# Attention on one core: the scores of two head pairs issued in a row, and value products that alternate between two PSUM banks in layers three and four

## The chip, the cores and the metric

The kernel runs on one core of one Trainium2 chip. The metric is the device time of one execution in microseconds (us); lower is better. The program is one launch, and its activations are only 256 tokens by 1024 columns, so most of its time goes to streaming and multiplying weights in TensorE.

## The reference

Two small transformer stacks are computed one after the other, four layers in all, on `x` of 1 x 256 x 1024 in fp32. The matrices around the attentions don't matter here. What matters is that each layer has attention over 256 tokens with heads of about 64 columns, and that this is computed per head:

```
s   = q @ k.T * scale + bias          # 256 x 256, causal or chunked
p   = exp(s - max(s))                 # row by row
out = (p @ v) / sum(p)
```

- Layer one ("nsa") has two branches of 16 heads each with one and the same mask (32 head jobs), and beside them a compressed branch. Each branch is weighted by a gate.
- Layer two ("dil") has 16 heads in three groups with three masks. The groups' weights come from the log sums of all heads.
- Layer three ("ab") has 8 heads with 96 rows of q and k (64 plain, 32 rotary), and then 8 heads of 64 with a sink in the denominator.
- Layer four ("cd") has 8 heads with 66 rows (64, and two that carry the forgetting decay), and then 8 heads of 64 with a bias table.

## The kernel before

Tokens lie in two tiles of 128. A head's scores are three blocks of 128 x 128 (the fourth is hidden by the mask), 384 columns in one PSUM bank. Heads go in pairs, and each engine has its own loop over pairs `p`:

- TensorE (`att_pe`, L611): scores of pair `p` (L641 and L643, `S` or `G0`/`G1` by the parity of `p`), transposes of pair `p-1`'s probabilities (`turn_probs`, L622, six of 128 x 128 in banks `T0`, `T1`), other work of the layer (`behind`), the value products of pair `p-2` (`times_v`, L630 to L632), and more work of the layer (`after`).
- VectorE (`att_dve`, L666): score plus bias with the row minimum of its negative, into one of four `scr` slots and `negmax` (L685, L687, "maxes"), then `between`, then the division of pair `p-2` by its sum (`take`: L2580 to L2588, L2248 to L2252, or L2242 to L2244), then `behind`.
- ScalarE (`att_act`, L708): the exponentials of pair `p` (L727, L728), `between`, then the copy of pair `p-1`'s transposes from PSUM (`copies`, L718), then `behind`.

A fp32 matmul is two instructions in the trace, so four stand for the scores of two heads. q and k of heads with 64 rows lie in one half of the partitions by the head's parity: the profile shows their matmuls as 64*128, those of the others as 96*128 or 66*128.

The order is held by semaphores. Scores of pair `p` wait for the maxes of pair `p-2`, which had the same banks. Maxes of pair `p` wait for the transposes of pair `p-2`, which had the same `scr` slots. The value products all go to bank `G2` (`out_bank`, L217; only the last pair but one uses `G3`), so those of a pair wait until `take` of the pair before is done (`att["outs"]`).

`G3` serves what `behind` and `after` bring in. In layer one these are the late parts of the modulation: L440 on TensorE, its sum on VectorE (L453), a spreading matmul (L446) and a copy on ScalarE (L458), in the iterations `LATE_AT = (2, 4, 7, 9, 11, 13)`; and the compressed branch: its maximum and probabilities on VectorE (L2552 to L2566), a transpose in iteration 5 (L1482, copied at L1999), and its outputs in `OUT_AT = (6, 8, 10, 12)` (L1493, L2574). ScalarE's `between` there scales a share of the late weights (L2015), and GpSimd adds them (L992). In its last iterations VectorE also splits the first quarter items of the next weights (L2609) from a copy by GpSimd (L1018), and GpSimd adds the branches (L986). Layer two has late parts in iteration 2 only. Layers three and four use `G3` in iterations 0 and 1 (`weave_turn`, L547).

Of the kernel before, what the change touches and what calls it, by code (L numbers as in the profile page):

```python
# [25 lines left out]
P = 128  # L26
D = 1024
T = 256
NT = T // P
KT = D // P  # L30
H = 16
# [24 lines left out]
SW = 3 * P  # L56
# [24 lines left out]
class Tally:  # L81
# [9 lines left out]
    def done(self, ins, sem=None):  # L91

        sem = self.own if sem is None else sem
        self.mark(ins, sem)
        self.eng.wait_ge(sem, self.n[sem.name] + (0 if self.turns is None else self.turns * self.per[sem.name]))
# [25 lines left out]
def over(ap, axis, n):  # L121

    a = ap.unsqueeze(axis)
    shape = list(a.shape)
    shape[axis] = n
    return a.broadcast_to(shape)


def two_stacks(nc, a, out):
    with ExitStack() as ctx:  # L130
# [83 lines left out]

        SB = [S, G[0:2]]

        def out_bank(name, p):  # L217

            return 3 if p == len(att_jobs[name]) // 2 - 2 else 2

        def att_out(name, j):
# [240 lines left out]
        turns = {}  # L462
# [145 lines left out]

        def att_pe(pe, name, behind=None, after=None, bank_free=None, mid=None):  # L611
            jobs, b0 = att_jobs[name], att_base[name]
            pairs = len(jobs) // 2

            def turn_probs(j):

                pe.wait_ge(att["probs"], 2 * (b0 + j) + 2)
                if j >= 2:

                    pe.wait_ge(att["turned"], b0 + j - 1)  # L620
                for b in range(3):
                    ins = pe.transpose(TB[j % 2][:, b * P:(b + 1) * P], scr[:, j % 4, 1 + b * P:1 + (b + 1) * P], ident)  # L622
                ins.then_inc(att["turns"], 1)

            def times_v(j):

                v = jobs[j][2]
                pe.wait_ge(att["turned"], b0 + j + 1)
                o, pt = att_out(name, j), probT[:, j % 4, :]
                pe.matmul(o[:, 0, :], pt[:, 0:P], v[0], start=True, stop=True)  # L630
                pe.matmul(o[:, 1, :], pt[:, P:2 * P], v[0], start=True, stop=False)  # L631
                pe.matmul(o[:, 1, :], pt[:, 2 * P:SW], v[1], start=False, stop=True).then_inc(att["pv"], 1)  # L632

            for p in range(pairs + 2):
                if p < pairs:
                    if p >= 2:

                        pe.wait_ge(att["maxes"], 2 * (b0 + 2 * (p - 1)))
                    two = [(jobs[2 * p + e][0], jobs[2 * p + e][1], SB[p % 2][e]) for e in range(2)]
                    for q, k, bank in two:  # L640
                        pe.matmul(bank[:, 0:P], q[:, 0:P], k[:, 0:P], start=True, stop=True)  # L641
                    for q, k, bank in two:
                        pe.matmul(bank[:, P:SW], q[:, P:T], k[:, 0:T], start=True, stop=True).then_inc(att["scores"], 1)  # L643
                if mid is not None:
                    mid(p)
                if p == pairs:
                    if bank_free is not None:
                        bank_free()
                    times_v(2 * p - 4)
                if 1 <= p < pairs + 1:  # L650
                    for j in (2 * p - 2, 2 * p - 1):
                        turn_probs(j)
                if p == pairs:
                    times_v(2 * p - 3)
                if behind is not None:
                    behind(p)
                if p >= 2 and p != pairs:
                    if p >= 3:

                        pe.wait_ge(att["outs"], b0 // 2 + min(p, pairs) - 2)  # L660
                    for j in (2 * p - 4, 2 * p - 3):
                        times_v(j)
                if after is not None:
                    after(p)

        def att_dve(dve, tl, name, bias_of, scale_of, take, sink=None, between=None, behind=None):  # L666
            done, TT = tl.done, dve.tensor_tensor
            jobs, b0 = att_jobs[name], att_base[name]
            n = len(jobs)
            for p in range(n // 2 + 2):  # L670
                for i in (2 * p, 2 * p + 1):
                    if i < n:
                        dve.wait_ge(att["scores"], b0 + i + 1)
                        if i >= 4:

                            dve.wait_ge(att["turns"], b0 + i - 3)
                        s, bank, bias, h = scr[:, i % 4, :], SB[p % 2][i % 2], bias_of(i), i % H
                        if i >= H:

                            dve.wait_ge(att["probs"], 2 * (b0 + i - H) + 2)  # L680
                        least, scale = 3e38, scale_of(i)
                        if sink is not None and sink(i) is not None:
                            least = sink(i)

                        tl.mark(dve.tensor_tensor_reduce(s[:, 1:1 + P], bank[:, 0:P], bias[:, 0:P], -scale, least, ALU.add, ALU.min,  # L685
                                                         negmax[:, h, 0:1]), att["maxes"])
                        tl.mark(dve.tensor_tensor_reduce(s[:, 1 + P:1 + SW], bank[:, P:SW], bias[:, P:SW], -scale, least, ALU.add, ALU.min,  # L687
                                                         negmax[:, h, 1:2]), att["maxes"])
                    if between is not None:
                        between(i)  # L690
                if sink is not None and 2 * p < n and sink(2 * p) is not None:
                    rows = slice(2 * p, 2 * p + 2)
                    dve.wait_ge(att["maxes"], 2 * (b0 + 2 * p + 2))
                    done(TT(den[:, rows, :], negmax[:, rows, :], over(sinks[:, 2 * p - 8:2 * p - 6], 2, NT), ALU.add), ab_s["sink_in"])
                if p >= 2:
                    dve.wait_ge(att["pv"], b0 + 2 * p - 2)
                    o, jobs_of = att_outs(name, p - 2), slice(2 * p - 4, 2 * p - 2)
                    rows = slice((2 * p - 4) % H, (2 * p - 4) % H + 2)
                    summed = o[:, :, :, DH:DH + 1]
                    if sink is not None and sink(2 * p - 4) is not None:  # L700
                        dve.wait_ge(ab_s["sink_exp"], p - 5)
                        summed = den[:, rows, :].unsqueeze(3)
                        done(TT(summed, summed, o[:, :, :, DH:DH + 1], ALU.add))
                    take(p - 2, o[:, :, :, 0:DH], summed, rden[:, jobs_of, :])
                if behind is not None:
                    behind(p)

        def att_act(act_, name, sink=lambda i: False, between=None, behind=None):  # L708
            n, b0 = len(att_jobs[name]), att_base[name]

            def copies(p):

                for j in (2 * p - 2, 2 * p - 1):
                    act_.wait_ge(att["turns"], b0 + j + 1)
                    if j >= 4:

                        act_.wait_ge(att["pv"], b0 + j - 3)
                    act_.copy(probT[:, j % 4, :], TB[j % 2][:, 0:SW]).then_inc(att["turned"], 1)  # L718

            for p in range(n // 2 + 1):  # L720
                if p == n // 2 - 1:
                    copies(p)
                for i in (2 * p, 2 * p + 1):
                    if i < n:
                        act_.wait_ge(att["maxes"], 2 * (b0 + i) + 2)
                        h, s = i % H, scr[:, i % 4, :]
                        act_.activation(s[:, 1:1 + P], s[:, 1:1 + P], ACT.Exp, bias=negmax[:, h, 0:1], scale=-1.0).then_inc(att["probs"], 1)  # L727
                        act_.activation(s[:, 1 + P:1 + SW], s[:, 1 + P:1 + SW], ACT.Exp, bias=negmax[:, h, 1:2],  # L728
                                        scale=-1.0).then_inc(att["probs"], 1)
                    if between is not None and i < n:  # L730
                        between(i)
                if p >= 1:
                    if p != n // 2 - 1:
                        copies(p)
                    if sink(2 * p - 2):
                        rows = slice(2 * p - 2, 2 * p)
                        act_.wait_ge(ab_s["sink_in"], p - 4)
                        act_.activation(den[:, rows, :], den[:, rows, :], ACT.Exp).then_inc(ab_s["sink_exp"], 1)
                if behind is not None:
                    behind(p)  # L740
# [2230 lines left out]
```

## Time and profile before

| What | us |
|---|---|
| median of 3 runs | 986.23 (985.34 to 986.41) |
| span of the profiled execution | 984.6 |
| attention of layer one | 108 to 182 |
| attention of layer two | 303 to 336 |
| attention of layer three | 412 to 441 |
| attention of layer four | 733 to 762 |

The span runs from the first to the last instruction; the page gives no time of the profiled execution beyond it, and the median of the runs is 1.6 us longer. In the views of the profile, PE is TensorE's matmuls and PEld its weight loads, DVE is VectorE, ACT ScalarE and POOL GpSimd. A row of a timeline has the start, the time from its first start to its last end, the engine and line, what is written from what, and in brackets the idle time before it with what ended it. Matmuls overlap in the pipeline: the step from one row's start to the next is what they cost, not the time in the second column.

### The profile page before, as it was taken

To read this page: it belongs to the slowest core of one execution; us is meant where nothing else is said; L and a number is where in the kernel's file an instruction comes from. 1 tells how busy PE (TensorE), PEld (TensorE's weight loads), DVE (VectorE), ACT (ScalarE), POOL (GpSimd) and SP (SyncE) were. 2 spreads that over 40 slices of the span, in tenths; PEclk is the share of its full clock that TensorE was granted. 3 is DMA by queue.
4 is the path that set the end of the run, shared out by engine and by line. 5 is a ranking of instruction groups with operands and counts; after the bars stand their busy time and mean duration, and the time that the engine had idled before them with its cause. 6 is when DMAs were issued, how large, how long until landed. Compare 5 with 4: busy or idle time off the path is not lost.

```text
span 984.6 us, 15103 instructions
## 1 busy us (share of the span) xinstructions
PE 954.9 (97%) x5656; PEld 806.3 (82%) x5656; DVE 645.7 (66%) x1164; ACT 471.4 (48%) x734; POOL 180.9 (18%) x154
## 2 busy tenths in 40 slices
PE   5999999999999999999999999999999999999996
PEld 2799666878886789988888888879999888888884
DVE  3656567975755775667766766676445776766665
ACT  1453577545445635573344444444457334444442
POOL 2015337204961301230000000010023000000001
PEclk9999999999999999999999999999999999999998
DMA  9865655435564255223465555534532336555541
GB/s 374 352 245 169 235 194 195 149 128 183 201 228 178 89 186 228 87 87 129 154 261 203 209 208 187 187 143 158 190 129 86 129 137 257 187 188 184 187 182 43
DMA packets 24105, 178.37 MB, mean 181 GB/s; under 512 B 3792, under 2 KB 4224, under 8 KB 7928
## 3 DMA queue, kind: packets, MB, share of 16 engines
q1 hardware_dynamic: 19840, 166.70, 45.4%
q0 software_dynamic: 2224, 8.94, 2.9%
q10 hardware_dynamic: 1991, 2.07, 0.8%
q8 instruction: 31, 0.51, 0.2%
q14 instruction: 19, 0.15, 0.0%
HBM read 176.65 MB, written 1.05 MB: 180 GB/s over the span
## 4 chain that ended last, share of the span: by engine, by line
PE 85%; DVE 9%; ACT 2%; DMA 2%; issue 1%; POOL 0%; SPq 0%; DVEq 0%; ACTq 0%; POOLq 0%
PE G L1109 12%; PE G L1111 12%; PE G L1110 12%; PE S L1229 8%; PE T L1229 8%; PE S L1228 4%; PE T L1228 3%; PE T L622 2%; PE T L527 2%; PE G L1309 2%; PE G L1298 2%; PE G L1290 2%; PE G L632 1%; PE G L631 1%; PE G L630 1%; DVE wlo L2174 1%
## 5 line engine op out<-in xcount | busy, mean ns | idle before, releaser
L2312 DVE TENSOR_TENSOR wlo<-ring,whi 128x2048 fp32r<-128x2048 f32 x88 | 154.4, 1758 | 88.4 <-ACT whi L1873 54.0
L1109 PE MATMUL G<-whi,hTh 128*128 128x308 f32 (+3 forms) x480 | 163.9, 341 | 0.5 <-DVE hTl L568 0.3
L1111 PE MATMUL G<-whi,hTl 128*128 128x308 f32 (+3 forms) x480 | 161.1, 336 | 0.0
L1110 PE MATMUL G<-wlo,hTh 128*128 128x308 f32 (+3 forms) x480 | 161.0, 336 | 0.0
L2174 DVE TENSOR_TENSOR wlo<-ring,whi 128x1024 fp32r<-128x1024 f32 (+3 forms) x66 | 105.4, 1635 | 64.9 <-ACT whi L1731 64.7
L1229 PE MATMUL S<-hT,whi 128*128 128x512 f32 x336 | 122.0, 397 | 0.0
L1229 PE MATMUL T<-hT,whi 128*128 128x512 f32 x336 | 120.6, 394 | 0.0
L1109 PEld LDWEIGHTS G<-whi,hTh 128*128 128x128 f32 x480 | 90.2, 188 | 11.2 <-DVE hTl L568 2.4
L1731 ACT CAST whi<-ring 128x1024 fp32r<-128x1024 f32 (+3 forms) x66 | 75.2, 1186 | 44.6 <-PE G L1111 30.1
L1868 ACT CAST whi<-ring 128x2048 fp32r<-128x2048 f32 x44 | 83.9, 1906 | 25.9 <-PE S L1332 17.5
L1110 PEld LDWEIGHTS G<-wlo,hTh 128*128 128x128 f32 x480 | 90.4, 188 | 5.7 <-issue 0.7
L1111 PEld LDWEIGHTS G<-whi,hTl 128*128 128x128 f32 x480 | 90.3, 188 | 5.0
L1228 PE MATMUL S<-hT,wlo 128*128 128x256 f32 x294 | 82.6, 281 | 0.0
L1878 ACT ACTIVATE sil<-gsum 128x256 f32<-128x256 f32 x44 | 18.4, 418 | 132.3 <-DVE gsum L2333 132.3
L1228 PE MATMUL T<-hT,wlo 128*128 128x256 f32 x294 | 81.3, 277 | 0.0
L1229 PEld LDWEIGHTS S<-hT,whi 128*128 128x128 f32 x336 | 63.1, 188 | 13.6 <-DVE wlo L2312 0.4
L1229 PEld LDWEIGHTS T<-hT,whi 128*128 128x128 f32 x336 | 63.0, 187 | 11.0
L937 POOL TENSOR_TENSOR rstd<-var,mhalf 128x1 f32<-128x1 f32 x18 | 11.6, 646 | 321.8 <-DVE var L2186 229.1
L1109 PE MATMUL G<-whi,acth 128*128 128x512 f32 x176 | 68.8, 391 | 0.4 <-DVE actl L2342 0.4
L1110 PE MATMUL G<-wlo,acth 128*128 128x512 f32 x176 | 68.5, 389 | 0.0
L1111 PE MATMUL G<-whi,actl 128*128 128x512 f32 x176 | 68.5, 389 | 0.0
L1873 ACT CAST whi<-ring 128x1024 fp32r<-128x1024 f32 x44 | 46.2, 1051 | 29.8 <-PE G L1111 29.8
(387 smaller groups left out, 1883.6 us busy)
## 6 DMA issues: line engine op xcount, KB each, us to landing
ring<-in_ffn SPq DMA_DIRECT2D x44, 1536.0 KB, 6.4
ring<-in_dil_w_in SPq DMA_DIRECT2D x16, 1024.0 KB, 4.8
ring<-in_cd_w_in SPq DMA_DIRECT2D x10, 1232.0 KB, 5.4
ring<-in_ada_w SPq DMA_DIRECT2D x12, 1024.0 KB, 6.6
early<-in_ada_w SPq DMA_DIRECT2D x8, 1024.0 KB, 10.1
ring<-in_nsa_w_in SPq DMA_DIRECT2D x5, 1432.0 KB, 7.4
ring<-in_ab_w_in SPq DMA_DIRECT2D x4, 1440.0 KB, 6.4
vec<-in_vecs POOLq DMA_DIRECT2D x11, 512.0 KB, 5.4
```

What stands on the lines that cost most here:

```text
L527: ins = pe.transpose(turn_bank(name, g)[0:width, n * P:(n + 1) * P], src, ident)
L622: ins = pe.transpose(TB[j % 2][:, b * P:(b + 1) * P], scr[:, j % 4, 1 + b * P:1 + (b + 1) * P], ident)
L1109: pe.matmul(out_, act_h, w_h, start=first_, stop=False)
L1110: pe.matmul(out_, act_h, w_l, start=False, stop=False)
L1111: return pe.matmul(out_, act_l, w_h, start=False, stop=last_)
L1228: pe.matmul(bank[:, 0:T], wlo[b][:, at], hT2[:, k, 0, :], start=False, stop=False)
L1229: ins = pe.matmul(bank[:], whi[b][:, at], hT2[:, k, :, :].rearrange("p h t -> p (h t)"), start=(k == 0), stop=(k == KT - 1))
L1731: sc_e.copy(whi[(k0 + j) % 2][:, at], raw[:, at]).then_inc(hi_done, 1)
L1868: sc_e.copy(whi[b][:, gu], ring[:, b, gu]).then_inc(st["gu_hi"], 1)
L1873: sc_e.copy(whi[b][:, dn], ring[:, b, dn]).then_inc(st["dn_hi"], 1)
L2174: TT(wlo[k % 2][:, at], raw[:, at], whi[k % 2][:, at].bitcast(F32), ALU.subtract).then_inc(lo_done, 1)
L2312: TT(wlo[b][:, part], ring[:, b, part], whi[b][:, part].bitcast(F32), ALU.subtract).then_inc(st[what + "_lo"], 1)
```

## The change

The three loops are written in another order. `scored_in` gives the pairs whose scores TensorE issues in iteration `p`: pair 0 in 0, pair 1 in 1, pairs 2 and 3 in 2, pairs 4 and 5 in 3, 6 and 7 in 5, and so on, and none in the even iterations above 2. VectorE does the maxes of pair `p+1` in iteration `p` from 3 on (pairs 2 and 3 in iteration 2, with `between` in between). ScalarE does the copies of pair `p-1` first and then the exponentials of pair `p+1`, then both `between`. In layers three and four value products go to `G3` for even pairs and `G2` for odd ones, and wait for the `take` of the pair before last.

```diff
+        TWO_BANKS = ("ab", "cd")
...
+            if name in TWO_BANKS:
+                return 3 - p % 2
             return 3 if p == len(att_jobs[name]) // 2 - 2 else 2
...
+        def scored_in(p, pairs):
+
+            if p < 2:
+                return (p,)
+            if p == 2:
+                return (2, 3)
+            return (p + 1, p + 2) if p % 2 == 1 and p + 2 < pairs else ()
...
+            def scores(p):
+
+                if p >= 2:
+
+                    pe.wait_ge(att["maxes"], 2 * (b0 + 2 * (p - 1)))
...
             for p in range(pairs + 2):
-                if p < pairs:
-                    if p >= 2:
-
-                        pe.wait_ge(att["maxes"], 2 * (b0 + 2 * (p - 1)))
...
+                for ahead in scored_in(p, pairs):
+                    scores(ahead)
...
+                    if name in TWO_BANKS:
+                        pe.wait_ge(att["outs"], b0 // 2 + pairs - 3)
                     times_v(2 * p - 4)
...
-                    if p >= 3:
+                    if name in TWO_BANKS and p >= 4:
+
+                        pe.wait_ge(att["outs"], b0 // 2 + p - 3)
+                    elif name not in TWO_BANKS and p >= 3:
...
                         pe.wait_ge(att["outs"], b0 // 2 + min(p, pairs) - 2)
```

In VectorE's loop (`att_dve`):

```diff
-            for p in range(n // 2 + 2):
+            def maxes(p):
+
                 for i in (2 * p, 2 * p + 1):
...
+            for p in range(n // 2 + 2):
+                if p <= 2:
+                    maxes(p)
+                elif p + 1 < n // 2:
+                    maxes(p + 1)
+                if between is not None:
+                    between(2 * p)
+                    between(2 * p + 1)
+                if p == 2:
+                    maxes(3)
                 if p >= 2:
                     dve.wait_ge(att["pv"], b0 + 2 * p - 2)
```

In ScalarE's loop (`att_act`), where `exps(p)` holds the four exponentials of pair `p` as they were:

```diff
             for p in range(n // 2 + 1):
-                if p == n // 2 - 1:
+                if p < 2:
+                    exps(p)
+                if p >= 1:
                     copies(p)
...
+                    if p + 1 < n // 2:
+                        exps(p + 1)
+                if between is not None and p < n // 2:
+                    between(2 * p)
+                    between(2 * p + 1)
                 if p >= 1:
-                    if p != n // 2 - 1:
-                        copies(p)
```

Lines move by the new text: L622, L630 to L632, L641 and L643 of before are L634, L642 to L644, L653 and L655 in the changed kernel.

TensorE in layer four before, from the last value product of iteration 5 through iteration 6 (`q2T` holds q and k of the 64 row heads):

```order
L632 MATMUL G2<-u_53,probT_63 128x65
L641 MATMUL G0<-q2T_56 128x128 [waits att_maxes]
L641 MATMUL G1<-q2T_56 128x128
L643 MATMUL G0<-q2T_56 128x256
L643 MATMUL G1<-q2T_56 128x256
L622 MATMUL T0<-tab_76,scr_62 128x128 [waits att_turned,att_probs]
```

The same engine and layer now, where the last pairs are scored:

```order
L644 MATMUL G3<-u_53,probT_63 128x65
L653 MATMUL S0<-q2T_56 128x128 [waits att_maxes]
L653 MATMUL S1<-q2T_56 128x128
L655 MATMUL S0<-q2T_56 128x256
L655 MATMUL S1<-q2T_56 128x256
L653 MATMUL G0<-q2T_56 128x128 [waits att_maxes]
L653 MATMUL G1<-q2T_56 128x128
L655 MATMUL G0<-q2T_56 128x256
L655 MATMUL G1<-q2T_56 128x256
L634 MATMUL T0<-tab_76,scr_62 128x128 [waits att_turned,att_probs]
```

One step from value products to scores and one from scores to transposes are gone, and the second pair's scores stand behind a wait for VectorE's maxes of the pair before.

TensorE in layer two now, iteration 4, between the value products of two pairs (bank `G2` for both):

```order
L644 MATMUL G2<-u_53,probT_63 128x65
L634 MATMUL T0<-tab_76,scr_62 128x128 [waits att_turned,att_probs]
L634 MATMUL T0<-tab_76,scr_62 128x128 x2
L634 MATMUL T1<-tab_76,scr_62 128x128 [waits att_turned,att_probs]
L634 MATMUL T1<-tab_76,scr_62 128x128 x2
L642 MATMUL G2<-u_53,probT_63 128x65 [waits att_turned,att_outs]
```

Before, the scores of a pair stood at this place too, ahead of the transposes; now only six transposes lie between the last product of one pair and the wait for its `take`.

VectorE in layer one now, end of iteration 3 and iteration 4 up to the late sum:

```order
L2615 RECIPROCAL rden_87<-G2 128x4 [waits att_pv]
L2616 TENSOR_TENSOR rden_87<-rden_87,gate_88 128x4 [waits dve_step]
L2619 TENSOR_TENSOR tok_50<-G2,rden_87 128x2x2x64 [waits dve_step]
L2597 TENSOR_TENSOR kT_55<-kT_55,tab_76 128x480 [waits nsa_cmp_exp,att_outs]
...
L706 ISA scr_62,negmax_85<-G0,tab_76 128x128 [waits att_turns,att_scores,nsa_cmp_prob]
...
L457 TENSOR_TENSOR mod0_77<-mod0_77,G3 128x512 [waits ada_late_part]
```

The rows have the same order as before; the maxes between the compressed probabilities (L2597 on, L2562 on before) and the late sum are those of pair 5 in place of pair 4.

## Rows read from the trace of the kernel before

**Rows 1.** Busy time of the engines, whole span (the page)
```profile
PE 954.9 (97%) x5656; PEld 806.3 (82%) x5656; DVE 645.7 (66%) x1164; ACT 471.4 (48%) x734; POOL 180.9 (18%) x154
```

**Rows 2.** Layers one and four by windows: busy time of each engine
```profile
core 0: us, PE busy (x) PEld busy (x) DVE busy (x) ACT busy (x) POOL busy (x), PEclk, DMA share, GB/s
108.00:182.00 74.00, 70.72 (x548) 49.11 (x549) 54.55 (x207) 54.67 (x128) 36.94 (x33) 1.00 0.50 188
...
733.00:762.00 29.00, 29.00 (x244) 26.51 (x242) 19.00 (x88) 22.08 (x54) 14.68 (x12) 1.00 0.33 109
```

**Rows 3.** TensorE in order of time, layer four, heads of 64 rows
```profile
start us, us, engine line op out<-in xcount [idle before <-releaser]
...
748.16 0.39 PE L632 MATMUL G<-u,probT 128*128 128x65 f32 x2
748.48 0.49 PE L641 MATMUL G<-q2T 64*128 64x128 f32 x4
...
749.34 0.87 PE L622 MATMUL T<-tab,scr 128*128 128x128 f32 x6
750.05 0.33 PE L630 MATMUL G<-u,probT 128*128 128x65 f32 x2
```

**Rows 4.** The same view, layer four, heads of 66 rows
```profile
738.87 0.61 PE L641 MATMUL S<-kT,qT 66*128 66x128 f32 x4
...
740.18 0.82 PE L622 MATMUL T<-tab,scr 128*128 128x128 f32 x6
```

**Rows 5.** The same view, last turns of layer four
```profile
757.90 0.82 PE L622 MATMUL T<-tab,scr 128*128 128x128 f32 x6
758.56 0.33 PE L630 MATMUL G<-u,probT 128*128 128x65 f32 x2
```

**Rows 6.** TensorE in order of time, layer two
```profile
309.25 0.89 PE L622 MATMUL T<-tab,scr 128*128 128x128 f32 x6 [0.53 <-ACT probT L718]
...
319.90 0.39 PE L632 MATMUL G<-u,probT 128*128 128x65 f32 x2
```

**Rows 7.** VectorE in order of time, layer two
```profile
320.33 0.18 DVE L2248 RECIPROCAL rden<-G 128x4 f32<-128x4 f32 x1 [0.64 <-PE G L632]
320.54 0.86 DVE L2252 SCALAR_TENSOR_TENSOR tok<-G,rden,u 128x64 f32<-128x64 f32 x4
```

**Rows 8.** TensorE in order of time, layer three
```profile
417.75 1.03 PE L643 MATMUL S<-kT,qT 96*128 96x256 f32 x4
418.92 0.90 PE L622 MATMUL T<-tab,scr 128*128 128x128 f32 x6
```

**Rows 9.** TensorE in order of time, layer one
```profile
116.63 1.92 PE L440 MATMUL G<-ring,cb 128*32 128x512 f32 x16 [0.87 <-DVE kT L2552]
...
129.34 1.12 PE L446 MATMUL G<-mod,ones 128*128 128x512 f32 x2 [0.45 <-DVE mod L453]
...
131.26 0.87 PE L622 MATMUL T<-tab,scr 128*128 128x128 f32 x6
...
135.72 0.89 PE L622 MATMUL T<-tab,scr 128*128 128x128 f32 x6 [1.01 <-ACT probT L718]
...
139.76 0.90 PE L622 MATMUL T<-tab,scr 128*128 128x128 f32 x6
...
167.38 0.89 PE L622 MATMUL T<-tab,scr 128*128 128x128 f32 x6 [0.22 <-ACT probT L718]
```

**Rows 10.** VectorE in order of time, layer one
```profile
124.81 0.66 DVE L2562 TENSOR_TENSOR kT<-kT,tab 128x480 f32<-128x480 f32 x1
...
134.11 1.26 DVE L2581 TENSOR_TENSOR rden<-rden,gate 128x4 f32<-128x4 f32 x1
```

**Rows 11.** VectorE by lines, layer one
```profile
line engine op names shapes xcount | busy us, mean ns | idle before us <-releasers
L687 DVE CUSTOM_DVE_ANT_0 scr<-G,tab 128x256 f32<-128x256 f32 x16 | 6.7, 421 | 0.0
...
L2581 DVE TENSOR_TENSOR rden<-rden,gate 128x4 f32<-128x4 f32 x15 | 6.5, 431 | 0.5
L685 DVE CUSTOM_DVE_ANT_0 scr<-S,tab 128x128 f32<-128x128 f32 x16 | 4.6, 290 | 2.5 <-PE S L643 2.4
```

**Rows 12.** ScalarE by lines, layer one
```profile
L727 ACT ACTIVATE scr<-scr,negmax 128x128 f32<-128x128 f32 x32 | 12.7, 396 | 14.9 <-DVE negmax L687 14.8
L2015 ACT ACTIVATE near<-near,cb 128x512 f32<-128x512 f32 x16 | 11.3, 706 | 0.0
```

More of the change, by code:

```diff
@@ L632, in times_v @@
                 pe.matmul(o[:, 1, :], pt[:, 2 * P:SW], v[1], start=False, stop=True).then_inc(att["pv"], 1)
-            for p in range(pairs + 2):
-                if p < pairs:
-                    if p >= 2:
-                        pe.wait_ge(att["maxes"], 2 * (b0 + 2 * (p - 1)))
[L639 to L643, printed above, removed]
+            def scores(p):
+                if p >= 2:
+                    pe.wait_ge(att["maxes"], 2 * (b0 + 2 * (p - 1)))
+                two = [(jobs[2 * p + e][0], jobs[2 * p + e][1], SB[p % 2][e]) for e in range(2)]
+                for q, k, bank in two:
+                    pe.matmul(bank[:, 0:P], q[:, 0:P], k[:, 0:P], start=True, stop=True)
+                for q, k, bank in two:
+                    pe.matmul(bank[:, P:SW], q[:, P:T], k[:, 0:T], start=True, stop=True).then_inc(att["scores"], 1)
+            for p in range(pairs + 2):
+                for ahead in scored_in(p, pairs):
+                    scores(ahead)
                 if mid is not None:
@@ L669, in att_dve @@
             n = len(jobs)
-            for p in range(n // 2 + 2):
+            def maxes(p):
                 for i in (2 * p, 2 * p + 1):
[L672 to L691, printed above, removed]
@@ new lines, in maxes @@
+                    dve.wait_ge(att["scores"], b0 + i + 1)
+                    if i >= 4:
+                        dve.wait_ge(att["turns"], b0 + i - 3)
+                    s, bank, bias, h = scr[:, i % 4, :], SB[p % 2][i % 2], bias_of(i), i % H
+                    if i >= H:
+                        dve.wait_ge(att["probs"], 2 * (b0 + i - H) + 2)
+                    least, scale = 3e38, scale_of(i)
+                    if sink is not None and sink(i) is not None:
+                        least = sink(i)
@@ new lines, in maxes @@
+                    tl.mark(dve.tensor_tensor_reduce(s[:, 1:1 + P], bank[:, 0:P], bias[:, 0:P], -scale, least, ALU.add, ALU.min,
+                                                     negmax[:, h, 0:1]), att["maxes"])
+                    tl.mark(dve.tensor_tensor_reduce(s[:, 1 + P:1 + SW], bank[:, P:SW], bias[:, P:SW], -scale, least, ALU.add, ALU.min,
+                                                     negmax[:, h, 1:2]), att["maxes"])
+                if sink is not None and sink(2 * p) is not None:
@@ L718, in copies, with exps @@
                     act_.copy(probT[:, j % 4, :], TB[j % 2][:, 0:SW]).then_inc(att["turned"], 1)
+            def exps(p):
+                for i in (2 * p, 2 * p + 1):
+                    act_.wait_ge(att["maxes"], 2 * (b0 + i) + 2)
+                    h, s = i % H, scr[:, i % 4, :]
+                    act_.activation(s[:, 1:1 + P], s[:, 1:1 + P], ACT.Exp, bias=negmax[:, h, 0:1], scale=-1.0).then_inc(att["probs"], 1)
+                    act_.activation(s[:, 1 + P:1 + SW], s[:, 1 + P:1 + SW], ACT.Exp, bias=negmax[:, h, 1:2],
+                                    scale=-1.0).then_inc(att["probs"], 1)
             for p in range(n // 2 + 1):
-                if p == n // 2 - 1:
+                if p < 2:
+                    exps(p)
+                if p >= 1:
                     copies(p)
[L723 to L731, printed above, removed]
+                    if p + 1 < n // 2:
[3 more added lines that the diff above has]
+                    between(2 * p + 1)
                 if p >= 1:
-                    if p != n // 2 - 1:
-                        copies(p)
                     if sink(2 * p - 2):
```

## Prediction

> **What bounds the kernel now.** I read the busy times first, then the attention stages by windows, then each engine's timeline inside them, and the lines with their idle time last. TensorE is busy for 97% of the span [rows 1], and inside the attentions for 70.7 of 74 us in layer one and all of 29 in layer four, at full clock (PEclk 1.00), while VectorE, ScalarE and GpSimd have room on average [rows 2]. So an edit pays here if it shortens what TensorE itself does, or removes one of the few waits; and it costs where it makes TensorE wait.
>
> What TensorE does can be shortened because its steps differ. In layer four, heads of 64 rows, the last row of value products starts at 748.16; such a row steps 0.22, so the next matmul is due at 748.38. The scores begin at 748.48 (0.10 late), the transposes at 749.34, the products at 750.05 [rows 3]. The six transposes there take 0.71, and 0.66 where they follow value products [rows 5]. So the scores of one pair cost 749.34 - 748.38 + 0.05 = 1.01. Heads of 66 rows, whose two jobs run one after the other over the full array, take 740.18 - 738.87 = 1.31 for the same columns [rows 4]. The 64 row jobs overlap (four matmuls of L641 in 0.49 [rows 3]), so their streaming part is about half of that, 0.66. The other 0.35 is the change into half arrays and back, with the pipeline filled anew.
>
> The Trainium skill (TensorEngine Tiling (Array Packing), Key Properties) says that a change of tiling mode drains TensorE. The trace agrees on both sides of it: late by 0.10 + 0.05 and more around 64*128 matmuls [rows 3], and no delay to speak of around 66*128 ones [rows 4]. By the rule alone, joined pairs of heads with 96 or 66 rows would give nothing, which is also how I count them from the rows.
>
> **Joined scores.** A second pair that follows in the same mode should cost 0.66 in place of 1.01: -0.35 for each joining. No row shows two such pairs in a row, so the bounds are 0 (the wait for maxes ahead of the second pair empties the pipeline as a change of mode would) and -0.35; I take -0.35, since the transposes too stand behind waits and step evenly. Joinings of 64 row heads: seven in layer one (2+3 to 14+15), three in layer two, and in layers three and four two each (4+5, 6+7); 2+3 there are wide heads and give 0.
>
> **Layer four.** 2 x -0.35 = -0.7. Nothing else is near. The second scores of a joining wait for the maxes of the pair before, four reductions of 0.29 and 0.42 [rows 11], some 1.15 with their overlap, from the transposes on; TensorE has value products (1.34, six steps of 0.22) and the first scores (0.66) in between, 2.0. The products now wait for the take of the pair before last, a whole iteration old.
>
> **Layer three.** Also -0.7. Besides, TensorE's transposes at 418.92 start later than 417.75 + 0.86 = 418.61 (the step of L643 for wide heads) [rows 8]: a hole of 0.3 that the scores of pair 3, now issued there, fill. -1.0.
>
> **Layer two.** Three joinings: -1.05. The transposes of iteration 2 wait 0.53 for a copy [rows 6]; the scores of pair 3 fill that: -0.5. Against it stands the one bank `G2`. The last row of products starts at 319.90, take starts at 320.33 and ends at 320.54 + 0.86 = 321.40 [rows 6, 7], so the next products can start at about 321.45. TensorE comes to them after 319.90 + 0.22 + 0.66 = 320.78 when only transposes lie between. That is a new wait of 0.67, in iterations 4, 6 and 7 (in 8 the products go to the other bank): +2.0. Before, a pair's scores covered it everywhere. Sum +0.45. Cost if the take is slowed: as much more.
>
> **Layer one.** Seven joinings would be -2.45, but here four engines are nearly tied, so I follow TensorE's starts.
>
> - Iteration 2: the wait of 0.87 at L440 for VectorE [rows 9] holds while scores of pair 3 are done under it (-0.65 or so for that pair).
> - Iterations 3 and 4: TensorE does scores 4 and 5 before transposes 2, so these start 0.65 later than before, and value products 1 with them. VectorE starts the compressed probabilities (124.81 [rows 10]) only after take 1, hence 0.65 later, and the late sum behind them releases L446, which waited for it already (129.34 [rows 9]). L446 at about 130.0, and after it scores 6 and 7 (0.66 more than one pair): transposes 4 at 132.5 instead of 131.26. TensorE is 1.25 later, but two pairs of scores ahead.
> - Iterations 5 and 6: the wait of 1.01 for copies [rows 9] goes, since ScalarE now copies first. In its place L1493 waits for the copy L1999, which stands on ScalarE behind exponentials and two scalings. Counted from the start of transposes 4, the maxes of pair 6 are done at 1.7, its exponentials at 2.65 (L727, 0.40, and L728, 0.5, of the second head), the scalings at 3.9 (0.71 each, overlapping a little [rows 12]), the copy at 4.4, where TensorE would be there at 3.2. Transposes 6 come 8.3 after transposes 4, against 139.76 - 131.26 = 8.5: 140.8.
> - Iterations 7 to 12, three rounds of two, each 9.2 before ((167.38 - 139.76) / 3 [rows 9]): the copy wait of 0.22 goes, a joining saves 0.35, and L1493 waits 0.2 for the late copy. 8.85 each, so transposes 12 at 167.3 (before 167.38), with all pairs scored.
> - Iterations 13 to 15: VectorE has a late sum, three splits and three takes there, in turn with GpSimd's copies, which stand behind its addition of the branch from take 11. That loop stays as long, and the two pairs of scores that TensorE no longer does in it (some 2.0) turn into waits for take 11 and take 12 in the one bank. At most 0.1 to 0.2 is won.
>
> Layer one: -0.2. If its chain were no hindrance it would be -2.45 - 0.87 - 0.22 x 4 and more, about -4; if each even iteration of the late part had to wait for a slow take, +2 (rival C). GpSimd's adds (L992) come some 2 us later behind ScalarE's scalings; I find them done just before the late sums and cost them at nothing, at risk of 0.3 in each of four.
>
> **Sum.** Against the span of 984.6: -0.2 + 0.45 - 1.0 - 0.7 = -1.45, so 983.2 for the span. The runs' median lies 1.6 above the span: 986.23 - 1.45 = 984.8. What follows an attention starts with TensorE busy, so the shift is kept.
>
> **Rivals.**
>
> A (the forecast): scores get cheaper, and about half of that goes to waits for the one output bank and for VectorE in layers one and two. 984.8, own range 983.7 to 985.9. Chance 0.50.
>
> B: layer one's chain gives way with TensorE. For it: before, TensorE was what ended most of VectorE's and ScalarE's waits (L727 idle 14.9 us in layer one lies behind maxes that lie behind scores). Then layer one gives -1.6 (four joinings of seven and the 0.2 waits), and the sum is -2.85: 983.4. With all seven, -3.7: 982.5. Chance 0.28.
>
> C, slower: takes of layer one grow. The small product L2581 beside GpSimd took 1.26 in one row [rows 10] and 0.43 in the mean [rows 11]; a take with 1.26 is 1.9 long, one with the mean 1.1. From a cover of 1.57 (transposes and L1493) between products, the wait is 0.3 + 1.9 + 0.05 - 1.6 = 0.65, for each of iterations 6, 8, 10, 12, and with the 1.0 that it adds to 14 and 15 it is 3.6. It decides from takes above 1.25 on. Against it: the mean of L2581 leaves takes at 1.1. 986.23 - 1.45 + 3.6 = 988.4. Chance 0.14, half of it below 988.2.
>
> D, the change doesn't do what it says: joined scores cost as much as single ones. Fourteen times 0.35 are lost, less what layer one would have lost to waits anyway (some 1.6): -1.45 + 4.9 - 1.6 = +1.85, 988.1. Against it: within a pair the half array matmuls of L641 and L643 step without a gap. Chance 0.08.
>
> **How the numbers follow.** What a measurement of this kernel can tell from no change is 0.2%, 2.0 us: below 984.26 is faster, above 988.2 slower. Faster: all of B and about a quarter of A, 0.40. Slower: half of C and less than half of D, 0.10. Same: 0.50. The range goes from B's far end to short of C: 982.6 to 987.4.
>
> **What would show it.** Right: two rows of scores (L653, L655) 0.66 apart in layers two to four; TensorE idle before L642 for VectorE's L2287 group in iterations 4, 6 and 7 of layer two, some 0.67 each; layers three and four without idle time and shorter by 1.0 and 0.7; in layer one the wait at L446 grown beyond 0.45, the wait of 1.01 gone, waits for takes in iterations 14 and 15, and a stage of the same length within 0.5. Wrong: layer one shorter by over 1 us, the second scores 1.0 after the first, or a stage after an attention that gives the gain back by waiting for weights.

## The result: 0.2 to 0.4% slower, and the profile after

The changed kernel took 989.94 us (median of 5, 989.68 to 990.72) against 986.23 (median of 5), a ratio of 1.0041 [1.0029, 1.0053]. In a second comparison (below) eleven executions of it had a median of 987.41, ratio 1.0021 [1.0010, 1.0033]. The forecast was 984.8 in 982.6 to 987.4. The profiled execution took 989.68, its span 987.9 in place of 984.6. The two rows that answer to [rows 1] and to the clock, from its page:

```profile
PE 955.3 (97%) x5656; PEld 810.5 (82%) x5656; DVE 645.0 (65%) x1164; ACT 472.3 (48%) x734; POOL 181.6 (18%) x154
...
PEclk9999989999999999999999999999999999999999
```

Work and instruction counts are as before; one slice of the clock's row, in layer one, is lower. To find the place, TensorE's instructions, in the same number and nearly the same order in both kernels, were compared start by start at the matmuls that the kernel before starts at 112, 298, 345, 412, 445, 690 and 770 us. In each stretch between two of these points (the first begins at 0) the changed kernel falls behind the one before by so much (us, profiled executions; minus where it gains; the forecast above it):

| | first 112 us | layer one | layer two | ahead of three | layer three | layer four |
|---|---|---|---|---|---|---|
| forecast | 0 | -0.2 | +0.45 | 0 | -1.0 | -0.7 |
| changed kernel | -0.74 | **+4.08** | +0.75 | -0.42 | +0.13 | -0.80 |

(From 445 to 690 it is +0.07.) Two columns are no effect of the change: all kernels below leave both stretches alone, and stand between -1.42 and +0.37 in the first and between -0.42 and +0.32 in the fourth.

**Layer four** does what was forecast. TensorE in order of time, heads of 64 rows, answering to [rows 3]:

```profile
747.35 0.49 PE L653 MATMUL S<-q2T 64*128 64x128 f32 x4
...
748.10 0.39 PE L653 MATMUL G<-q2T 64*128 64x128 f32 x4
...
748.86 0.87 PE L634 MATMUL T<-tab,scr 128*128 128x128 f32 x6
```

From the first scores to the transposes it was 0.86 for one pair in [rows 3]; it is 1.51 for two, so the second costs 0.65 (forecast 0.66). A pair alone costs 1.01, since 0.10 ahead of its scores and 0.05 in the transposes behind them go with it.

**Layer two** too: three new waits for VectorE's take of the one bank, 0.5 idle each where 0.67 was forecast (from the view of TensorE's waits, 298 to 345 us; in total, times, longest):

```profile
PE G L642 <- DVE tok L2287: 1.5, 3, 0.5
```

**Layer one** has three waits of 1.4 us (the same view, 115 to 190 us), and behind each the granted clock is down in the windows, where the kernel before had 1.00 in all of them:

```profile
PE G L450 <- DVE mod L457: 1.4, 1, 1.4
PE G L1528 <- issue: 1.4, 1, 1.4
PE G L642 <- DVE tmp L2623: 1.4, 1, 1.4
```

```profile
core 0: us, PE busy (x), PEclk, DMA share, GB/s
...
130.00:135.00 5.00, 5.00 (x32) 0.68 0.00 0
...
140.00:145.00 5.00, 5.00 (x36) 0.66 0.50 152
...
180.00:185.00 5.00, 5.00 (x33) 0.66 0.00 0
```

In windows of 1 us the first fall reads 0.50, that is 1.2 GHz in place of 2.4, from 130 to 133. What it does to the double block of scores (TensorE in order of time):

```profile
129.29 1.58 PE L450 MATMUL G<-mod,ones 128*128 128x512 f32 x2 [1.45 <-DVE mod L457]
130.80 0.80 PE L653 MATMUL S<-kT,qT 64*128 64x128 f32 x4
131.39 1.06 PE L655 MATMUL S<-kT,qT 64*128 64x256 f32 x4
132.25 0.64 PE L653 MATMUL G<-kT,qT 64*128 64x128 f32 x4
132.67 0.88 PE L655 MATMUL G<-kT,qT 64*128 64x256 f32 x4
133.48 0.87 PE L634 MATMUL T<-tab,scr 128*128 128x128 f32 x6
```

130.80 to 133.48 is 2.68 for two pairs; the same block took 1.51 in layer four. The first matmul behind the wait (L450, 129.29) starts before the fall: the window from 129 to 130 still reads 0.91. Behind the third wait, which ends at 178.66, the windows of 1 us read 1.00 until 181: a fall is to be looked for in the us behind a wait, not in the next row alone.

**Layer three** lost its gain to another thing. GpSimd, VectorE and TensorE in order of time:

```profile
428.54 2.36 POOL L1075 TENSOR_TENSOR out_lo<-ring,wlo 128x1024 fp32r<-128x1024 f32 x1
...
429.35 1.57 DVE L713 TENSOR_TENSOR den<-negmax,small 128x4 f32<-128x4 f32 x1
...
431.64 0.35 DVE L706 CUSTOM_DVE_ANT_0 scr<-G,bias,negsink 128x128 f32<-128x128 f32 x1
...
433.13 0.49 PE L653 MATMUL G<-q2T 64*128 64x128 f32 x4 [1.01 <-DVE negmax L708]
```

The sum of the sinks, four elements per row, took 1.57 us and ended at 430.92, GpSimd's subtraction at 430.90. The three later sums of the same line, with GpSimd done, took 0.16 or 0.17. The maxes of pair 5 come behind it, and the second pair of the joining waits 1.01 for them.

### The profile page after: what moved, and what is told of

Its sections match the earlier page's. It is cut to its first block, busy times and chain, and to the rows that moved or that the text cites. A ratio compares the mean times of both kernels' runs of the same rounds, so it can differ in the third digit from the quotient of the medians.

```text
span 987.9 us, 15107 instructions
## 1 busy us (share of the span) xinstructions
PE 955.3 (97%) x5656; PEld 810.5 (82%) x5656; DVE 645.0 (65%) x1164; ACT 472.3 (48%) x734; POOL 181.6 (18%) x154
## 4 chain that ended last, share of the span: by engine, by line
PE 88%; DVE 8%; DMA 2%; issue 1%; ACT 1%; POOL 0%; SPq 0%; DVEq 0%; ACTq 0%; POOLq 0%
PE G L1144 12%; PE G L1146 12%; PE G L1145 12%; PE S L1264 8%; PE T L1264 8%; PE S L1263 4%; PE T L1263 3%; PE T L634 2%; PE G L1344 2%; PE G L1333 2%; PE G L1325 2%; PE T L531 2%; PE G L644 2%; PE G L642 2%; PE G L643 2%; DVE wlo L2209 1%
```

## The experiments

All times are medians. The kernel before was measured again beside each group of kernels: 985.93 for the first two questions, 986.13 for the third, and for the fourth 985.72 (feed-forward) and 986.23 (layer four). The stage numbers are read from one profiled execution each, as in the table above.

**First question: is it the clock, and is it layer one?** Three matmuls of 512 columns, whose result nobody reads, were put into each of the three waits:

```diff
+ if p == 4:
+     pe.wait_ge(att["turned"], 8)
+     keep_busy(3, TB[0])
...
```

(and likewise ahead of the compressed output in iteration 6 and of the products in iteration 15.) Expected:

> The changed kernel with twelve hundred columns or so of spare matmul work put into its three new holes in layer one (three 512 column matmuls of 0.48 us each against the identity, written to a PSUM bank whose content has been read: ahead of L450 in iteration 4, ahead of L1528 in iteration 6, ahead of the value products in iteration 15). The holes are 1.45, 1.44 and 1.38 us long in the changed kernel's trace, and right behind each the matmuls take about twice as long for 3.5 to 4 us. Theory one (the clock): the time is lost because TensorE's granted clock falls behind these holes, and four matmuls of scores for two pairs take 2.7 us there and not 1.49. With the holes filled the clock stays at full speed although the work is more: layer one 4 to 4.5 us shorter than in the changed kernel, total 985.5 to 986.2, clock 0.996 and not 0.992. Theory two (the waits alone): what is lost is the waiting for VectorE and ScalarE; filling it changes nothing, 989.9, or makes it up to 0.5 longer.

Measured: 988.72 (7 executions), 1.0029 [1.0017, 1.0040], clock 0.996 to 0.998 in every one, against 0.992 to 0.993. The clock is right by T1, the time is not: the fillers outlast the waits they fill. The first one reads (TensorE, layer one)

```profile
127.26 2.79 PE L1167 MATMUL T<-tab 128*128 128x512 f32 x6
```

2.79 us for a wait of 1.45: the expectation counted 0.48 for each of the three matmuls, but in fp32 each is two instructions (x6). Against a kernel with the same layer one whose clock did not fall (below) the three cost 0.92, 0.90 and 0.93, 2.7 in all. So the total doesn't decide between the two theories; layer one is 1.2 shorter than in the changed kernel's profile (+2.88 against +4.08), with 2.7 of filling in it. A filler must be shorter than the hole.

Layer one in its old order, all else as changed:

```diff
+ OLD = ("nsa",)
  def scored_in(p, pairs, name):
+     if name in OLD:
+         return (p,) if p < pairs else ()
...
```

(VectorE's and ScalarE's loops take their old order for `OLD` in the same way.)

> The changed kernel with layer one alone in the order of before on all three engines; layers two to four as changed. The changed kernel lost 4.1 us between the start and the end of layer one against the kernel before. Theory one (layer one's new order is the whole loss): 989.9 - 4.1 = 985.8, that is within 0.5 of before, because layer two gives +0.7, layer three +0.1, layer four -0.7. Theory two (the loss in layer one only shows a slack that would come up later): over 987. TensorE's clock 0.996.

Measured: 985.38 (11 executions), 0.9994 [0.9985, 1.0003]; layer one +0.26, layer two +0.47, layer three +0.17, layer four -0.80. As expected by its first theory. The whole loss is in layer one's new order.

**Second question: what costs layers two and three?** The sum of the sinks one iteration later:

```diff
  for p in range(n // 2 + 2):
      ... maxes(p) or maxes(p + 1), between(...)
+     if p < n // 2:
+         sink_sum(p)
```

> The changed kernel, where in layer three VectorE adds the sink to the row minimum of a pair (L713, 128 x 4) one iteration later, behind the maxes of the next pair. In the changed kernel this small sum took 1.57 us once, beside GpSimd's split, and the maxes of pair 5 came late, so that TensorE waited 1.01 us ahead of the scores of pair 7 and entered half array mode anew (0.35). Theory one: that one sum is why layer three gained nothing; with it out of the way layer three is 1.1 to 1.4 us shorter, 988.6 to 988.9. Theory two: the slow small operation only moves to another one on VectorE (the next small product), and the wait stays: 989.6 to 990.0.

Measured: layer three -1.23 in place of +0.13, by 1.36 as T1 has it. VectorE there now:

```profile
429.10 0.48 DVE L708 CUSTOM_DVE_ANT_0 scr<-G,bias,negsink 128x256 f32<-128x256 f32 x1
429.50 0.16 DVE L716 TENSOR_TENSOR den<-negmax,small 128x4 f32<-128x4 f32 x1
```

The total, 986.20 (11 executions, 985.02 to 988.84), is far below the expected one, and that was not the sinks: layer one gave +2.49 in this profile with the same code. Its executions fall apart by their mean clock: 988.5 to 988.8 at 0.992 to 0.993 (one at 986.3), 986.1 to 986.3 at 0.994, 985.0 to 985.6 at 0.996 and 0.997. In the profiled one (0.994) the clock fell only behind the third wait, but for about twice as long as in the changed kernel (0.50 from 177 to 183 in windows of 1 us):

```profile
175.00:180.00 5.00, 5.00 (x30) 0.64 0.00 0
180.00:185.00 5.00, 5.00 (x29) 0.68 0.38 125
```

Layer two on two banks as well, from its third pair on:

```diff
- if name in TWO_BANKS:
+ if name in TWO_BANKS or (name == "dil" and p >= 2):
      return 3 - p % 2
```

> The changed kernel, with layer two too alternating its value products between two banks, from pair 2 on (behind a wait for the last late part, which is over by then). Theory one (the single bank costs layer two three waits of 0.51 idle, 0.67 in all each): layer two is 2.0 us shorter, 987.9, and no idle time stands ahead of its value products. Theory two (VectorE's takes are late by themselves and the waits move to the end of the layer, where the group sums stand): 1 us or less, 988.9 to 989.9.

Measured: 987.58 (11 executions), 1.0014 [1.0005, 1.0023]; layer two -1.50 in place of +0.75, 2.25 less (2.0 expected), and the waits of L642 there are gone. Its profiled execution was the one of eleven with a clock of 0.998 (984.45; eight at 0.991 to 0.992 took 987.4 to 988.7), so it shows layer one as changed without a fall. Windows and TensorE in order of time, at the places shown for the changed kernel:

```profile
130.00:135.00 5.00, 4.59 (x37) 1.00 0.22 88
...
140.00:145.00 5.00, 5.00 (x44) 1.00 0.61 190
...
180.00:185.00 5.00, 4.76 (x33) 1.00 0.38 113
```

```profile
130.41 1.12 PE L450 MATMUL G<-mod,ones 128*128 128x512 f32 x2 [0.93 <-DVE mod L457]
131.46 0.49 PE L653 MATMUL S<-kT,qT 64*128 64x128 f32 x4
...
132.97 0.87 PE L634 MATMUL T<-tab,scr 128*128 128x128 f32 x6
...
137.67 1.10 PE L1530 MATMUL G<-rotk,kT 120*128 120x512 f32 x2 [1.44 <-issue]
...
141.49 0.87 PE L634 MATMUL T<-tab,scr 128*128 128x128 f32 x6
...
176.55 0.44 PE L642 MATMUL G<-u,probT 128*128 128x65 f32 x2 [1.38 <-DVE tmp L2625]
```

The waits are there, the falls are not, and layer one costs +0.18 in place of +4.08. From the first wait's end to the transposes it is 2.56 us here and 4.19 in the changed kernel, from the second's to the next even transposes 3.82 and 5.43, and the third fall costs 0.7: 3.9 together, the whole difference. (With the shift of the first 112 us taken off, L450 starts at 130.0 in both, so that the first wait is 0.93 and not 1.45 costs nothing here.) The kernel with the sinks moved, whose one fall was the long one, stands at +2.49: that fall cost 2.3.

**Third question: do the causes of the waits go?** The changed kernel ran again beside one in which three pieces of layer one's work are moved:

```diff
- elif p == 3:
+ elif p == 4:
      compressed_prob()          # VectorE: behind the maxes
...
+ if i == 10:
+     pcT_copy()                 # ScalarE: ahead of the scalings
...
+ if p in (13, 14, 15):
+     low_quarter(p - 13)        # VectorE: behind the take
```

(The comments are put in here; the old places of the last two are taken out.)

> The changed kernel, unchanged, beside the others of this call and with the clock of each execution. Known so far: its five executions all had a mean granted clock of 0.992 to 0.993 and 989.7 to 990.7 us, while the kernels that keep its layer-one order but differ behind layer one had 0.994 or 0.998 in some executions and were 1.3 to 3.9 us shorter in those than in their others. T1 (the waits of about 1.4 us in layer one are each a chance of a fall of TensorE's clock, and the clock is what the change loses): the executions fall into groups by their mean clock; 0.992 goes with 989.5 to 990.7 us, 0.994 with 987.5 to 989, and one at 0.998, if there is one, with 985.7 to 986.7. Median 989.0 to 990.2. T2 (the loss is the same work taking longer, and the clock only goes with it): all executions within 0.8 us of one another whatever their clock.

> Changed kernel; in layer one three pieces of work are moved so that TensorE does not wait for them: the sum of the compressed probabilities on VectorE one iteration later (behind the maxes), the copy that the compressed output's product waits for ahead of ScalarE's scalings of that pair, and the quarters of the low factor behind the takes of outputs in the last three iterations. Everything else as changed. T1 (the waits, through the clock and their own idle time, are the loss in layer one): no wait over 1.2 us between 115 and 190 us, the clock 1.00 in that whole stretch, 0.996 to 0.998 over the kernel in every execution, layer one 2 to 5 us shorter than in the changed kernel's profile (+4.07 against the kernel before becomes +2 to -1), total 985.0 to 987.5. T2 (the joined scores themselves are the loss: two pairs' scores in a row bring the clock down or hold up VectorE): the drops stay, 989 to 990.5. T3 (the moved pieces only move the waits to other places, as VectorE's and ScalarE's work per round is the same): waits of the same sum elsewhere, 987.5 to 990.

Measured, changed kernel again: eleven executions, three at a clock of 0.992 with 989.9 to 990.8 us, seven at 0.994 or 0.995 with 986.4 to 987.8 but for one of 989.5, one at 0.996 with 987.0. None reached 0.998. T1's groups are there, the middle one a us below where T1 had it, and one execution stands outside them; the median, 987.41, is 1.6 below T1's range, since fewer executions fell into the slow group than in the first comparison. T2 is out. The same code is a kernel of about 987 or of 990 us. The profiled execution (987.41) has the same three waits of 1.4 us and one fall, behind the first, and its layer one gives +1.94: with none, one and three such falls in the profile the same layer one stands at +0.18 (the kernel with two banks), +1.94 and +4.08. Moved pieces: 984.14 (11 executions, 983.46 to 985.09), 0.9982 [0.9973, 0.9991], clock 0.996 to 0.998 in all, layer one -1.62. The time is better than T1's range, and T1's sign that no wait over 1.2 us is left did not come. The waits of TensorE between 115 and 200 us:

```profile
PE S L531 <- DVE tok L2632: 1.4, 1, 1.4
PE G L642 <- DVE tmp L2627: 0.8, 1, 0.8
PE G L1517 <- DVE kT L2605: 0.5, 1, 0.5
```

The waits at L450 and L1528 are gone or short; one of 1.4 stands at the stage's end (177 us), and the clock stayed at 1.00 behind it. The joined scores are all still there, so they alone don't bring the clock down.

Two kernels put the pieces together:

> Three edits together: layer one in its old order, the sum of the sinks one iteration later in layers one and three, and the two accumulator banks in layer two as well (from its third pair on). From the pieces measured alone: layer one 0, layer two -1.5 (layer two with two banks, against +0.74 with one), layer three -1.1 (from +0.14), layer four -0.74, the stretch ahead of layer three -0.4. Sum about -3.5 to -3.8 against the kernel before: 982.3 to 982.8 if the pieces add up (T1); 983.5 to 985 if later idle time takes part of them back (T2). Clock 0.996 to 0.998.

> As the kernel with the three moved pieces in layer one, with the sum of the sinks one iteration later and layer two on two banks besides. If the moved pieces free layer one (T1), this is that kernel's time less 1.2 (layer three) and less 2.2 (layer two): 981.6 to 984.1. If they don't, 985 to 987. In either case it stands 3 to 3.8 us under the kernel with the three moved pieces alone.

Measured: 981.61 (5 executions), 0.9956 [0.9943, 0.9970], stages +0.07, -1.74, -1.24, -0.80; and 981.05 (5 executions), 0.9946 [0.9932, 0.9960], stages -1.60, -1.50, -1.23, -0.78. The first is a little better than T1; in its profiled execution (981.32) the first 112 us, which it leaves alone, stood at -1.42. The second is a little below T1's range (981.6 to 984.1), 3.1 under the kernel with the moved pieces alone (3 to 3.8 expected), and beats both the kernel before and the changed one by 5 us or more. The two aren't told apart by these runs.

**Fourth question: what does it take for the clock to fall?** Waits of chosen length were put into the kernel before. TensorE waits until GpSimd, idle there, has zeroed a free tile; first twice in the last steps of the second feed-forward:

```diff
+ gap(down(1, FF_STEPS - 3, False, ((0, 0), (0, 1), (1, 0))), 1)
...
+ gap(down(0, FF_STEPS - 2, False, ((0, 0), (0, 1), (1, 0))), 2)
...
# GpSimd, twice:
+ pool.wait_ge(gap_go, n + 1)
+ pool.memset(bias8[:, 0:650], 0.0).then_inc(gap_over, 1)
```

> The kernel before, with two waits put into TensorE's last two steps but one of the second feed-forward (about 945 and 953 us, where the engine ran without a pause at 1.00): ahead of the last quarter of a product it waits until GpSimd has set 650 columns of a free tile to zero. By the rows of such sets (0.31 us for 256 columns, 2.66 for 3072) one takes 0.65 us; with the two hand-overs some 0.9 to 1.1 us of idle time each. T1 (what counts is how long TensorE stands still: the kernel before came through a wait of 1.01 us without a fall): +1.8 to +2.2 us, the clock of all executions as before (0.996 to 0.998), 987.8 to 988.4. T2 (any such wait is a chance of a fall, short or long): some executions at 0.994 or 0.992 and 2 to 5 us longer.

> The same two waits with 1110 columns: 1.05 us of setting, some 1.3 to 1.5 us of idle time each, as long as the three of layer one in the changed kernel. T1 (a wait of this length is where the clock begins to fall, in some executions and not in others, whatever the work around it): the executions spread over clocks of 0.998 to 0.992; 988.7 to 989.2 us at 0.998 and 2 to 4 us more where it fell. T2 (what brought the clock down in layer one is the work there, narrow products with many changes of operand, and not the wait alone; in the dense stretch it stays): all at 0.996 to 0.998, 988.7 to 989.2.

> The same two waits with 1800 columns: 1.65 us of setting, some 1.9 to 2.1 us of idle time each. T1 (a longer stand makes the fall certain): every execution with two falls, clock 0.991 to 0.993, time 986 plus 4.0 for the waits plus 3 to 5 for the clock, 993 to 995. T2 (the waits alone cost): 989.8 to 990.4 at 0.996 to 0.998.

Measured: waits of 0.76, 1.14 and 1.72 us, +2.1, +2.6 and +3.2 us, clock 0.997 or 0.998 in all 28 executions. The waits cost about their own length (twice 0.76, 1.14, 1.72, that is 1.5, 2.3 and 3.4): T1 for the shortest, T2 for the two longer ones, which came out shorter and so cheaper than expected. That the clock held is read from the windows in the three profiled executions, and in the others from the mean clock. The longest, and the window around it (TensorE):

```profile
964.10 0.50 PE L1114 MATMUL G<-whi,acth 128*128 128x512 f32 x1 [1.72 <-POOL bias L1097]
```

```profile
960.00:965.00 5.00, 3.29 (x15) 1.00 0.00 0
```

Then three times in layer four, among the attention's narrow products, in the old order of scores:

```diff
+ if name == "cd" and j in (4, 8, 12):
+     first_.then_inc(gap_go, 1)
+     pe.wait_ge(gap_over, j // 4)
...
```

> The kernel before with three waits put into TensorE's layer four (old order of scores), in iterations 4, 6 and 8, behind the first value product of a pair: it waits until GpSimd, idle there, has set 640 columns of a spare tile to zero twice. From the 0.64 us of one such set and 0.12 us around it: 1.4 to 1.5 us each. T1 (a wait of this length among the attention's narrow products is what lets the clock fall, in some executions and not in others, while the dense feed-forward came through waits of 0.76, 1.14 and 1.72 us at 1.00): executions between 0.998 and 0.992; 990.0 to 990.6 us without a fall, 1 to 4 us more with falls. T2 (it is something of layer one itself, and not attention's products beside a wait): every execution at 0.996 to 0.998, 989.8 to 990.6.

> The same three waits with three sets each, 2.1 us of idle time. T1: the falls are more frequent than with 1.4 us; mean clock at or under 0.994 in most executions, 993 to 997 us. T2: 0.996 to 0.998 in every one, 992.0 to 992.8.

Measured: 996.20 (6 executions, clock 0.985 to 0.993) and 998.88 (4 executions, 0.989 to 0.991), more than T1 had. The first of them, TensorE in order of time and by windows:

```profile
748.47 0.44 PE L637 MATMUL G<-u,probT 128*128 128x65 f32 x2 [2.25 <-POOL gapt L1099]
757.62 0.44 PE L637 MATMUL G<-u,probT 128*128 128x65 f32 x2 [1.44 <-POOL gapt L1099]
763.55 0.61 PE L637 MATMUL G<-u,probT 128*128 128x65 f32 x2 [1.43 <-POOL gapt L1099]
```

```profile
750.00:755.00 5.00, 5.00 (x34) 0.66 0.25 105
755.00:760.00 5.00, 3.56 (x30) 1.00 0.00 0
760.00:765.00 5.00, 3.57 (x27) 0.87 0.00 0
765.00:770.00 5.00, 5.00 (x27) 0.50 0.02 3
```

Layer four is 12.2 us longer with 5.1 of idle time (the first wait was 2.25 because GpSimd was still at its last split). The other 7.1 are the work done at 1.2 GHz and what follows from it: in windows of 1 us the clock is at 0.50 from 751 to 753 and from 764 to 773, and what is missing to full speed adds up to 6.8 us. The clock fell behind the first wait (2.25) and the third (1.43) and not behind the second (1.44); the second fall reached into the 512 column products behind the attention. In the other kernel, with waits of 2.95, 2.12 and 2.12, it fell at all three. So the falls need neither layer one nor joined scores: a wait of 1.4 us among narrow products can be enough. The feed-forward and the layer four kernels ran on different chips, and the falls of layer one were seen on two more, so a difference between chips isn't excluded as a part of the contrast.

## Why the prediction was wrong

- **Layer one, the term that failed (-0.2; measured +4.08, and +1.94 in the repetition).** The walk along TensorE's starts was right: with the shift of the first 112 us taken off, L450 starts at 130.0 (forecast 130.0), and where the clock held, the even transposes stand at 132.6, 141.1 and 167.5 against 132.5, 140.8 and 167.3; the rounds of iterations 7 to 12 take 8.8 (8.85). The step that failed is the price of the waits that it left. Each grown wait (L446, the late copy at L1493, the take in iteration 15) was priced by its idle time, and the work behind it at the durations that [rows 9] show, all of them from a trace with a clock of 1.00. Behind a wait of 1.4 us the clock fell to half in all three places of the changed kernel's profile, 3.9 us: all but 0.4 of the difference between -0.2 and +4.1. No rival of the prediction held this. Rival C had +3.6 for the same stage by slow takes; the number is near, but the mechanism is not: no take of iterations 6 to 12 held TensorE up.
- **What was to be seen ahead.** The profile before had 1.01 us as the longest wait inside layer one [rows 9], at full clock; that nothing longer was in it was no evidence that longer ones are harmless.
- **Layer three, the second failed term.** The saving was there (-1.23 with the sum of the sinks out of the way), but the condition put beside it, maxes of "some 1.15 with their overlap", left out a small sum between two pairs' maxes that stands still beside GpSimd's splits. It cost 1.36. A small product that took 1.26 beside GpSimd was in [rows 10] (L2581), and was used only for rival C. The Trainium skill (SBUF — State Buffer, Who interferes with whom) says that a VectorE instruction with two inputs in SBUF contends with a GpSimd instruction that reads SBUF; the trace agrees, to the 0.02 us between the ends of L1075 and L713.
- **Layer two** (+0.45, measured +0.75 and +0.47 in two kernels) and **layer four** (-0.7, measured -0.80) are right in mechanism and, within 0.3, in size. The joining saves 0.36 (0.35).
- **Layer one's gain.** That the chain gives joined scores nothing is right: +0.18 in the one profile without a fall. It was not a law: with three pieces moved it is -1.62.

Without falls and with the sinks moved the change would sum to 0.18 + 0.75 - 1.23 - 0.80 = -1.1, near the forecast's -1.45. As it stands it is +0.3 without falls and +4.2 with three (0.18 or 4.08 + 0.75 + 0.13 - 0.80).

Open is why the same wait is followed by a fall in one execution and not in the next: with waits of 1.3 to 1.45 us at the same three places (one of 0.93 with two banks), the clock fell behind three in the changed kernel's profile, behind one in its repetition, one with the sinks moved and none with two banks. The Trainium skill (TensorE: Matmul & The Clock Gate, HAM oscillation — how this bites in real kernels) names idle gaps between matmuls as what brings the clock down again; these traces agree in kind, and show it at gaps shorter than those of its example. What in the feed-forward protects it, the width of its products or its fullness before the wait, wasn't tried apart.

## What to carry to other kernels

When an edit moves idle time of TensorE into fewer and longer waits, price the work behind each wait at both clocks, above all among narrow products, and look at the clock of every execution and not at one profile. Look next for what the wait waits for: three pieces of work on other engines, moved by an iteration or less, gave 3.3 us (987.41 to 984.14), while spare matmuls gave the clock back and took 2.7 us for it. Between two reductions on VectorE, don't leave a small operation with two SBUF inputs while GpSimd reads SBUF.

## What the runs showed of the hardware

- The granted clock fell from 2.4 to 1.2 GHz behind waits of 1.4 us among narrow products in some executions and not in others, costing 0.7 to 2.3 us each in layer one; behind the waits of 0.93 and 1.01 in the profiles at hand it did not.
- Behind waits of up to 1.72 us in the dense feed-forward the mean clock stayed at 0.997 or 0.998 in 28 executions (six of them with the longest).
- The same kernel took 986.4 to 990.8 us in eleven executions, in step with its mean clock (0.996 to 0.992) but for one of them.
- Two pairs of 64 row scores in a row take 1.51 against 0.86 for one (0.65 more), and a pair alone costs 1.01 with its 0.15 around it: going into half arrays and back costs 0.36.
- A VectorE sum of 128x4 with two SBUF inputs took 1.57 us beside a GpSimd subtraction that reads SBUF, and 0.16 us away from it.
